# Gate and up units of four FFNs: one 512-column product for the high weights, and the up half's scale moved to the down sums

## What is computed

```python
def rms_norm(x, g):
    xf = x.astype(jnp.float32)
    y = xf * lax.rsqrt(jnp.mean(xf * xf, axis=-1, keepdims=True) + EPS)
    return (y * g.astype(jnp.float32)).astype(x.dtype)

def swiglu(h, w_gate, w_up, w_down):
    return (jax.nn.silu(h @ w_gate) * (h @ w_up)) @ w_down
...
        h = rms_norm(x, ffn1_norm[layer])
        x = x + 0.5 * swiglu(h, ffn1_w_gate[layer], ffn1_w_up[layer], ffn1_w_down[layer])
```

## Time and profile before

| | |
|---|---|
| median of 3 runs | 1409.77 us (1407.46 to 1409.8) |
| the profiled execution's own time | 1410.74 us |
| its span, first to last instruction | 1409.0 us |
| TensorE busy | 1358.9 us (96%), 9241 products |
| VectorE busy | 921.1 us (65%) |
| ScalarE busy | 664.5 us (47%) |
| GpSimd busy | 141.6 us (10%) |
| mean DMA rate | 163 GB/s |
| granted TensorE clock, mean over the span | 0.985 of full speed |

### The profile page before, as it was taken

How to read it: one execution, slowest core, us unless ns; L and a number is a source line. 1 busy time by engine, 2 the same in 40 slices (tenths; PEclk the granted TensorE clock), 3 DMA queues, 4 the chain that set the end, 5 groups by cost and what they waited for, 6 DMA issues and landing times.

```text
span 1409.0 us, 23055 instructions
## 1 busy us (share of the span) xinstructions
PE 1358.9 (96%) x9241; PEld 1250.9 (89%) x9241; DVE 921.1 (65%) x1220; ACT 664.5 (47%) x867; POOL 141.6 (10%) x131
## 2 busy tenths in 40 slices
PE   7999998899999999999999999999988999899996
PEld 7999987679999999999998889999988988899995
DVE  5655567688755566555567676555668668866666
ACT  6434453565433454433467664443445443455542
POOL 1100003107500000000014310000003100000000
PEclk9999999899999999999999999999999999999998
DMA  7755643215655646555544346565522244365550
GB/s 263 222 179 182 196 145 134 56 60 179 220 181 180 192 135 216 194 187 179 183 147 150 120 164 209 183 192 191 179 90 91 90 141 159 132 198 189 193 183 30
DMA packets 164372, 229.30 MB, mean 163 GB/s; under 512 B 3995, under 2 KB 133274, under 8 KB 164192
## 3 DMA queue, kind: packets, MB, share of 16 engines
q1 hardware_dynamic: 162064, 221.33, 48.7%
q0 software_dynamic: 2160, 7.24, 1.7%
q10 hardware_dynamic: 96, 0.02, 0.0%
HBM read 227.52 MB, written 1.05 MB: 162 GB/s over the span
## 4 chain that ended last, share of the span: by engine, by line
PE 85%; DVE 9%; issue 2%; ACT 2%; POOL 1%; DMA 0%; ACTq 0%; DVEq 0%
PE ps L349 26%; PE ps L350 25%; PE ps L351 25%; DVE w_lo L291 2%; PE ps L2081 1%; PE ps L1184 1%; POOL p_sb L1270 1%; PE ps L1877 1%; ACT w_hi L283 1%; PE ps L534 1%; DVE h_lo L570 1%; PE ps L391 0%; PE ps L411 0%; ACT h_hi L553 0%; PE ps L393 0%
## 5 line engine op out<-in xcount | busy, mean ns | idle before, releaser
L291 DVE TENSOR_TENSOR w_lo<-raw,w_hi 128x2048 fp32r<-128x2048 f32 x208 | 484.3, 2330 | 149.4 <-ACT w_hi L283 149.2
L349 PE MATMUL ps<-h_hi,w_hi 128*128 128x256 f32 x1904 | 540.3, 284 | 1.3 <-DVE w_lo L291 0.6
L350 PE MATMUL ps<-h_hi,w_lo 128*128 128x256 f32 x1904 | 538.7, 283 | 0.0
L351 PE MATMUL ps<-h_lo,w_hi 128*128 128x256 f32 x1904 | 538.7, 283 | 0.0
L283 ACT ACTIVATE w_hi<-raw 128x2048 fp32r<-128x2048 f32 x208 | 397.4, 1912 | 272.3 <-PE ps L351 271.9
L349 PEld LDWEIGHTS ps<-h_hi,w_hi 128*128 128x128 f32 x1904 | 365.1, 192 | 4.4 <-issue 1.0
L350 PEld LDWEIGHTS ps<-h_hi,w_lo 128*128 128x128 f32 x1904 | 365.2, 192 | 1.8
L351 PEld LDWEIGHTS ps<-h_lo,w_hi 128*128 128x128 f32 x1904 | 365.2, 192 | 0.0
L349 PE MATMUL ps<-w_hi,gu_hi 128*128 128x512 f32 x400 | 156.3, 391 | 0.1
L350 PE MATMUL ps<-w_hi,gu_lo 128*128 128x512 f32 x400 | 156.2, 391 | 0.0
L351 PE MATMUL ps<-w_lo,gu_hi 128*128 128x512 f32 x400 | 155.7, 389 | 0.0
(11 more groups left out here) (309 smaller groups left out, 1562.8 us busy)
## 6 DMA issues: line engine op xcount, KB each, us to landing
raw<-in_ffn_w_up_dram SPq DMA_DIRECT2D x44, 1024.0 KB, 5.4
raw<-in_ffn_w_down_dram SPq DMA_DIRECT2D x44, 1024.0 KB, 4.9
raw<-in_ffn_w_gate_dram SPq DMA_DIRECT2D x43, 1024.0 KB, 5.4
raw<-in_w_up_dram SPq DMA_DIRECT2D x22, 1024.0 KB, 5.1
raw<-in_w_in_dram SPq DMA_DIRECT2D x14, 1024.0 KB, 5.4
raw<-in_odd_w_qkv_dram SPq DMA_DIRECT2D x12, 1024.0 KB, 5.1
raw<-in_w_down_dram SPq DMA_DIRECT2D x11, 1024.0 KB, 5.1
raw<-in_even_w_in_dram SPq DMA_DIRECT2D x6, 1024.0 KB, 5.1
```

The costliest lines, as they stand in the source:

```text
L291: dve.tensor_tensor(w_lo[slot][:, :], raw[slot][:, :], w_hi[slot][:, :].bitcast(F32), ALU.subtract).then_inc(w_lo_ready, 1)
L349: mm(o, ahi, bhi, start=first, stop=False)
L350: mm(o, alo, bhi, start=False, stop=False)
L351: return mm(o, ahi, blo, start=False, stop=last)
```

## The change

`h_hi` and `h_lo` become one tensor, `h_both`. A gate or up unit of the four FFNs becomes `wide_unit`: for each half t, 8 products of `w_hi` with 512 moving columns, the 256 of `h_hi` and then the 256 of `h_lo`, into a bank of its own (gate banks 0 and 1, up banks 2 and 3); then for each half 8 products of `w_lo` with the 256 columns of `h_hi`, added to the first 256 columns of the same bank. The first 16 wait for `w_hi` alone, the other 16 for `w_lo`. The sums now lie in two pieces, columns 0 to 255 and 256 to 511. ScalarE copies the second pieces of both banks to SBUF (`act_second_halves`), and VectorE adds the first pieces to them (`add_halves`). `scale` is done for the gate half only, in SBUF. The up half is left without rs, which goes into the factor of the down sums: rs_half = 0.5·rs, one column of scalars, in place of 0.5. In the last step of each FFN `gu_hi` and `gu_lo` go ahead of the split of the next unit. The conv FFN and the mixers are as before.

```diff
-        h_hi = sb("h_hi", [P, KC, S], F32R)
-        h_lo = sb("h_lo", [P, KC, S], F32R)
+        h_both = sb("h_both", [P, 2, KC, S], F32R)
+        h_hi, h_lo = h_both[:, 0], h_both[:, 1]
...
+        def wide_hi(pe, slot, t, bank, ks):
+
+            a = feat_view(w_hi[slot])
+            for k in ks:
+                pe.matmul(PS[:, bank, :], a[:, k, t * P:(t + 1) * P], h_both[:, :, k, :],
+                          start=k == 0, stop=False, skip_group_check=True)
+
+        def wide_lo(pe, slot, t, bank, ks):
+
+            b = feat_view(w_lo[slot])
+            for k in ks:
+                last = pe.matmul(PS[:, bank, 0:S], b[:, k, t * P:(t + 1) * P], h_hi[:, k, :],
+                                 start=False, stop=k == KC - 1, skip_group_check=True)
+            return last
+
+        def wide_unit(pe, n, bank, i=0, between=None):
+
+            slot = n % RING
+            pe.wait_ge(w_hi_ready, 3 * i + (n + 1))
+            for t in range(2):
+                wide_hi(pe, slot, t, bank + t, range(KC))
+            if between is not None:
+                between(pe)
+            pe.wait_ge(w_lo_ready, 3 * i + (n + 1))
+            for t in range(2):
+                last = wide_lo(pe, slot, t, bank + t, range(KC))
+            last.then_inc(w_released, 1)
...
+                ks = range(4 * half, 4 * half + 4)
+                for k in ks:
+                    norm.ready(pe, k)
+                    wide_hi(pe, slot, 0, 0, (k,))
+                wide_lo(pe, slot, 0, 0, ks)
+                if norm.at and half == 0:
+                    norm.pe_turn(pe, 3)
+                wide_hi(pe, slot, 1, 1, ks)
+                last = wide_lo(pe, slot, 1, 1, ks)
...
-                        pe.wait_ge(self.gate_scaled if which == 0 else self.up_scaled, free + self.b)
-                feat_unit(pe, n, which, i, between=between)
+                        pe.wait_ge(self.gate_added if which == 0 else self.up_added, free + self.b)
+                if self.conv:
+                    feat_unit(pe, n, which, i, between=between)
+                else:
+                    wide_unit(pe, n, 2 * which, i, between=between)
+
+            def act_second_halves(self, act, which, at):
+
+                act.wait_ge(w_released, self.u0 + 1 + which + at)
+                o = (ffn_act, ffn_up)[which].rearrange("p (t s) -> p t s", t=2)
+                act.activation(o, PS[:, 2 * which:2 * which + 2, S:2 * S], ACT.Copy)                   .then_inc((self.gate_second, self.up_second)[which], 1)
+
+            def add_halves(self, dve, which, i):
+
+                dve.wait_ge((self.gate_second, self.up_second)[which], i + (self.b + 1))
+                o = (ffn_act, ffn_up)[which].rearrange("p (t s) -> p t s", t=2)
+                dve.tensor_tensor(o, PS[:, 2 * which:2 * which + 2, 0:S], o, ALU.add)                   .then_inc((self.gate_added, self.up_added)[which], 1)
...
-                if not first:
+                last = isinstance(i, int) and i == FF_STEPS - 1
+                split_first = self.conv or not last
+                if not first and split_first:
                     split_hi(act, u + 6, i=r)
...
+                if not split_first:
+                    split_hi(act, u + 6, i=r)
...
+                    self.add_halves(dve, 0, i)
                     if first:
                         self.norm.wait_wide(dve)
-                    dve.wait_ge(w_released, u + 1 if first else u + 3 * r + 3)
-                    self.norm.scale(dve, ffn_act.rearrange("p (t s) -> p t s", t=2),
-                                    PS[:, 0, :].rearrange("p (t s) -> p t s", t=2)).then_inc(self.gate_scaled, 1)
+                    dve.wait_ge(self.gate_added, i + (self.b + 1))
+                    gate = ffn_act.rearrange("p (t s) -> p t s", t=2)
+                    self.norm.scale(dve, gate, gate).then_inc(self.gate_scaled, 1)
...
-                    self.norm.scale(dve, ffn_up.rearrange("p (t s) -> p t s", t=2),
-                                    PS[:, 1, :].rearrange("p (t s) -> p t s", t=2)).then_inc(self.up_scaled, 1)
-                    dve.wait_ge(self.up_scaled, i + (self.b + 1))
+                    self.add_halves(dve, 1, i)
+                    dve.wait_ge(self.up_added, i + (self.b + 1))
...
+                    dve.tensor_scalar(rs_half[:, :], rs_tok[:, :], 0.5, None, ALU.mult).then_inc(self.half_ready, 1)
...
-                        m = dve.scalar_tensor_tensor(x, y, 0.5, x, ALU.mult, ALU.add)
+                        m = dve.scalar_tensor_tensor(x, y, rs_half[:, tb:tb + 1], x, ALU.mult, ALU.add)
...
-        after_out = dict(banks=(2, 3, 4, 5), lo_after={2: [0, 1], 3: [2, 3]})
+        ffn_after_ffn = dict(banks=(2, 3, 4, 6), lo_after=after_ffn["lo_after"], wide_bank=4)
+        after_out = dict(banks=(2, 3, 4, 5), lo_after={2: [0, 1], 3: [2, 3]}, wide_bank=4)
```

More of the change, by code:

```diff
@@ L166, in build @@
         rs_tok = sb("rs_tok", [P, TB])
+        rs_half = sb("rs_half", [P, TB])
         rs_wide = nc.alloc_sbuf_tensor_at("rs_wide", [P, S], F32, offset=place["fox_k_lo"])
@@ L397, in feat_unit_first, with wide_unit_first @@
             last.then_inc(w_released, 1)
+        def wide_hi(pe, slot, t, bank, ks):
[20 more added lines that the diff above has]
+            last.then_inc(w_released, 1)
+        def wide_unit_first(pe, n, norm):
+            slot = n % RING
+            if n == 0:
+                pe.wait_ge(start_lo, 1)
+            else:
+                pe.wait_ge(w_lo_ready, n + 1)
+            for half in range(2):
+                if n == 0 and half == 1:
+                    pe.wait_ge(w_lo_ready, 1)
+                ks = range(4 * half, 4 * half + 4)
[7 more added lines that the diff above has]
+                last = wide_lo(pe, slot, 1, 1, ks)
+            last.then_inc(w_released, 1)
         def feat_unit_halves(pe, n, bank, norm):
@@ L507, in build, with __init__ @@
             wide_ready = sem("late_wide_ready")
-            def __init__(self, at, second_unit, gain, banks, wides, lo_after, early_split=False):
+            def __init__(self, at, second_unit, gain, banks, wides, lo_after, early_split=False, wide_bank=3):
                 self.at, self.second_unit, self.banks, self.early_split = at, second_unit, banks, early_split
-                self.gain, self.wides, self.lo_after = gain, wides, lo_after
+                self.gain, self.wides, self.lo_after, self.wide_bank = gain, wides, lo_after, wide_bank
             def x_wait(self, eng, q):
@@ L601, in act_wide @@
                 act.wait_ge(self.wide_turned, self.wides)
-                act.activation(rs_wide[:, :], PS[:, 3, 0:S], ACT.Copy).then_inc(self.wide_ready, 1)
+                act.activation(rs_wide[:, :], PS[:, self.wide_bank, 0:S], ACT.Copy).then_inc(self.wide_ready, 1)
             def wait_wide(self, eng):
@@ L671, in build @@
         class Ffn:
+            gate_added = sem("ffn_gate_added")
             gate_scaled = sem("ffn_gate_scaled")
-            up_scaled = sem("ffn_up_scaled")
+            up_added = sem("ffn_up_added")
+            gate_second = sem("ffn_gate_second")
+            up_second = sem("ffn_up_second")
+            half_ready = sem("ffn_half_ready")
             act_done = sem("ffn_act_done")
@@ L713, in pe @@
                 else:
-                    feat_unit_first(pe, u, 0, self.norm)
+                    wide_unit_first(pe, u, self.norm)
                     self.up(pe, u + 1, 1, 0, None, between=self.norm.pe_wide)
@@ L787, in act_step @@
                     self.conv_tap2(act, 0, i, at_g)
+                else:
+                    self.act_second_halves(act, 0, at_g)
                 split_hi(act, u + 3 if first else u + 5, i=r)
@@ L793, in act_step @@
                 else:
+                    self.act_second_halves(act, 1, at_u)
                     act.wait_ge(self.gate_scaled, i + (self.b + 1))
                     act.activation(ffn_act, ffn_act, ACT.Silu).then_inc(self.act_done, 1)
-                if not first:
+                last = isinstance(i, int) and i == FF_STEPS - 1
+                split_first = self.conv or not last
+                if not first and split_first:
                     split_hi(act, u + 6, i=r)
                 act.wait_ge(self.gu_done, i + (self.b + 1))
-                last = isinstance(i, int) and i == FF_STEPS - 1
                 if not first and not last:
@@ L853, in dve_step @@
                    .then_inc(self.gulo_done, 1)
+                if not split_first:
+                    split_lo(dve, u + 6, i=r)
             def dve(self, dve, then=None, following=None):
                 self.dve_step(dve, 0, True)
+                if not self.conv:
+                    dve.tensor_scalar(rs_half[:, :], rs_tok[:, :], 0.5, None, ALU.mult).then_inc(self.half_ready, 1)
                 with dve.Fori(0, FF_STEPS - 2) as i:
@@ L860, in dve @@
                 self.dve_step(dve, FF_STEPS - 1, False)
+                if not self.conv:
```

(3 more changed lines are left out.)

4 lines of the change are left out of this document (2 added, 2 removed).

## The result

Four runs of each kernel, in turn on one chip: 1408.62 us (1404.41 to 1409.8) before, 1388.41 us (1386.87 to 1390.25) after, a ratio of 0.9862 (0.9837 to 0.9887). The forecast was 1393.9, its range 1390.5 to 1399.5: the kernel gained 20.2 us, 15.9 were forecast. The profiled execution took 1390.25 us.

The account below looks back on a forecast made before the run. TensorE's product issue was taken to bound the FFNs. FFN gains of 4.3, 4.2, 4.2 and 3.2 us sum to 15.9, so 1410.74 becomes 1394.8, and 1393.9 us as median; range 1390.5 to 1399.5.

Parts of the forecast that it names:

- The fixed part, 17.6 us from 88 units: Gate and up units of the four FFNs: each product removed saves a fixed 12.5 ns, 0.20 us a unit.
- rivals 2 and 3: Two-piece wide product dearer than 0.2275 us: 8.8 us less gain, 1402.7 (0.06); or above 0.239 us, kernel slower, 1425.6 (0.03).
- Rival 4: A removed product gives back a fifth of its 12.5 ns: 3.5 us come back, 1408 us; chance 0.03.
- (a) gate0: Start of each FFN: gate0's second half waits for the next norm's `h_lo`, 0.1 us lost per FFN.
- (b): Gate1 reuses gate0's banks and waits for its add: a tie, 0.1 us in each FFN but the first.
- (c): Start of `ffn2_0`, beside GpSimd: up1 waits for up0's add, first four units give nothing, 0.4 us lost; stage gives 3.2.
- The sum's last line: The FFNs' 15.9 us off the profiled 1410.74 gives 1394.8; the median 1.0 lower, so 1393.9 us.

Follow-up runs that it names:

- narrow: The changed kernel with each 512-column product of `w_hi` issued as two of 256 columns: 1408.73 us, ratio 1.0001 to the kernel before.
- gate_only: The changed kernel with wide products in gate units only, those of up units issued as two of 256 columns: 1398.44 us, ratio 0.9925 to before.
- interleaved: The changed kernel with each `w_lo` product right behind the wide one of the same k, not in rows: 1400.01 us, ratio 0.994 to before.
- base_late10: The kernel before with 10 filler products behind gate0 of `ffn1_1`, shifting everything after it: 1407.86 us, ratio 0.9992 to before.
- wide_late6: The changed kernel with 6 filler products behind gate0 of `ffn1_1`: 1395.27 us, ratio 0.9893 to the kernel before.
- wide_late10: The changed kernel with 10 filler products behind gate0 of `ffn1_1`: 1395.05 us, ratio 0.99 to the kernel before.
- base_late5: The kernel before with 5 filler products behind gate0 of `ffn1_1`: 1407.7 us, ratio 0.9993 to before.

## Why the prediction was right and where it failed

- *The fixed part, 17.6 us from 88 units.* Right in size: the step is 16.58 us as forecast, and narrow and gate_only show the gain to be that of the wide products, in proportion. The two pieces of the moving operand cost nothing that shows; rivals 2 and 3 are out. Rival 4 is out too: the stages gave 15.9 us. By the gap formula in the Trainium skill, "TensorE: Matmul & The Clock Gate", section "Back-to-back issue gap", which that section gives for isolated products, the estimate was 3.5 us for the removed ones; the measurement goes against it here.
- *The reason for it* was half wrong. I took 12.5 ns as a property of any product. In interleaved, with as few products, only half of it comes back. That the forecast's step came out rests on the new order keeping the wide products in rows, which the sum did not know to matter.
- *(a) gate0.* TensorE waits 0.22 us for `h_both` in the second half at `ffn2_0`, where it waited 0.19 for `h_lo` before: the wait is as laid out, but it grew by less than the 0.1 booked. *(b)*: a tie was booked at 0.1 us an FFN; it costs nothing. *(c)*: the waits of 0.96 and 0.49 us came at the two places named (1 to 1.5 had been expected for the first); `ffn2_0` gave 3.45 where 3.2 was forecast. The FFNs together: 15.9 forecast, 15.9 measured (4.3 + 3.45 + 4.2 + 3.9).
- *The sum's last line is the step that failed.* It took everything outside the four FFNs at zero and the median's scatter at 1.2 us. There, 4.5 us more came in the traces. By the means the gain is 19.6 us, 3.7 beyond the FFNs' 15.9, and the clock's share, an upper estimate, fell by 4.4. The granted clock of 0.985 in the table of before said that the lower clock takes up to 0.015 × 1409 = 21 us, some 5 of them at the end, where TensorE is idle and nothing is lost. The rest lies in stages that the change shifts by 4 to 18 us. That term was missing, in the sum and in the range. Put at ± 5 us, as base_late10 and wide_late6 now show it, the range would have begun near 1385.5. Of the 5.5 us between the forecast and the median after, 1.15 are none of the change's: the sum started from 1409.77, the median of three runs, and before had 1408.62 beside the changed kernel.
- *What stays open.* That placement moves the time of either kernel by 3 to 6 us through the clock is shown, and 1.35 us of filler is enough to take the changed kernel's advantage in the clock away ((1 − clock) × time is 20.2 us in wide_late6, 15.5 without the filler, 19.9 before). Which placements are good is not: the picture by which wide_late10 was to match base_late5 is wrong or incomplete. The second mixer is never hit (123.6 to 123.7 us in all 18 traces), and TensorE's waits in it are short; that these two belong together fits, but no run tests it.
